# Norm chains moved behind the block boundary, and unread matmuls in TensorE's waits

## What is computed

```python
a = rms_norm(h, g) * (1 + scale) + shift        # before each of the four sub-layers
layer 0: h += gate * rwkv7_mixer(a)             # bidirectional linear recurrence, 16 heads
         h += gate * swiglu(a', w1, w3, w2)     # d_ff 2816, latent and context tokens
layer 1: h += gate * gqa_attention(a)           # 8 query heads, 2 key heads, rotary
         h += gate * swiglu(a', w1, w3, w2)     # latent tokens only
rms_norm(x, g) = x * rsqrt(mean(x * x) + 1e-6) * g
```

## Time and profile before

| | |
|---|---|
| median of 3 runs | 2176.03 us (2170.07 to 2177.54) |
| profiled execution | 2173.98 us, its span 2172.1 us |
| TensorE matmul busy | 1988.3 us (92%) |
| VectorE (DVE) busy | 1230.3 us (57%) |
| ScalarE (ACT) busy | 836.8 us (39%) |
| GpSimd (POOL) busy | 379.3 us (17%) |
| mean granted TensorE clock | 0.963 of 2.4 GHz |

### The profile page before, as it was taken

How to read it: one execution, slowest core, us unless ns; L and a number is a source line. 1 busy time by engine, 2 the same in 40 slices (tenths; PEclk the granted TensorE clock), 3 DMA queues, 4 the chain that set the end, 5 groups by cost and what they waited for, 6 DMA issues and landing times. The chain is left out here.

```text
span 2172.1 us, 52627 instructions
## 1 busy us (share of the span) xinstructions
PE 1988.3 (92%) x22423; PEld 1739.4 (80%) x22423; DVE 1230.3 (57%) x1921; ACT 836.8 (39%) x1407; POOL 379.3 (17%) x394
## 2 busy tenths in 40 slices
PE   5799997789999988979999999997979898999998
PEld 3688886678888887979999999996635476888887
DVE  4765445667767763458756667564775434333333
ACT  2433334565565532344323324233335424422321
POOL 0000000766766652120000000022200010000000
PEclk8799998899999999989999999997989998999999
DMA  9577775101111001411212222212100023333332
GB/s 318 180 239 231 228 237 144 41 19 39 32 39 39 20 12 47 151 59 59 78 59 78 63 74 69 68 39 69 59 20 1 0 68 96 96 105 89 96 107 79
DMA packets 226985, 192.76 MB, mean 89 GB/s; under 512 B 13386, under 2 KB 211668, under 8 KB 226388
## 3 DMA queue, kind: packets, MB, share of 16 engines
q1 hardware_dynamic: 226452, 188.84, 28.1%
q0 software_dynamic: 320, 0.79, 0.2%
HBM read 171.38 MB, written 17.43 MB: 87 GB/s over the span
## 5 line engine op out<-in xcount | busy, mean ns | idle before, releaser
L539 DVE TENSOR_TENSOR ffn_lo<-ffn_raw,ffn_hi 128x1024 fp32r<-128x1024 f32 (+1 forms) x58 | 77.5, 1336 | 196.0 <-ACT ffn_hi L534 196.0
L563 PE MATMUL banks<-operand_hi,ffn_w_hi 128*128 128x384 f32 x464 | 155.7, 336 | 10.9 <-DVE operand_lo L505 10.9
L563 PE MATMUL banks<-operand_lo,ffn_w_hi 128*128 128x384 f32 x464 | 155.6, 335 | 0.0
L563 PE MATMUL banks<-operand_hi,ffn_w_lo 128*128 128x384 f32 x464 | 155.5, 335 | 0.0
L563 PE MATMUL banks<-mix_hi,proj_hi 128*128 128x386 f32 (+1 forms) x384 | 136.9, 356 | 15.4 <-DVE proj_lo L755 10.5
L563 PE MATMUL banks<-operand_hi,ffn_hi 128*128 128x512 f32 x352 | 138.4, 393 | 10.7 <-DVE operand_lo L505 8.4
L534 ACT CAST ffn_hi<-ffn_raw 128x1024 fp32r<-128x1024 f32 (+1 forms) x60 | 68.3, 1139 | 189.6 <-PE banks L563 182.6
L563 PE MATMUL banks<-operand_lo,ffn_hi 128*128 128x512 f32 x352 | 137.9, 392 | 0.0
L563 PE MATMUL banks<-operand_hi,ffn_lo 128*128 128x512 f32 x352 | 137.9, 392 | 0.0
L430 POOL TENSOR_TENSOR mix_and_norm<-mix_and_norm 128x768 f32<-128x768 f32 (+1 forms) x21 | 34.8, 1659 | 572.4 <-ACT mix_and_norm L424 572.4
L563 PE MATMUL banks<-mix_hi,proj_lo 128*128 128x386 f32 (+1 forms) x384 | 132.0, 344 | 0.0
(11 more groups left out here) (341 smaller groups left out, 5681.4 us busy)
## 6 DMA issues: line engine op xcount, KB each, us to landing
mod_raw<-in_mod_w SPq DMA_DIRECT2D x96, 512.0 KB, 5.2
ffn_raw<-in_ff_w SPq DMA_DIRECT2D x32, 1024.0 KB, 5.3
ffn_raw<-in_ff_w SPq DMA_DIRECT2D x46, 512.0 KB, 3.8
ffn_raw<-in_ff_w SPq DMA_DIRECT2D x16, 704.0 KB, 4.7
proj_raw<-in_rw_wr SPq DMA_DIRECT2D x16, 256.0 KB, 5.3
proj_raw<-in_rw_wk SPq DMA_DIRECT2D x16, 256.0 KB, 6.1
proj_raw<-in_rw_wv SPq DMA_DIRECT2D x16, 256.0 KB, 6.1
rwkv_out_raw<-in_rw_wo SPq DMA_DIRECT2D x8, 512.0 KB, 4.2
```

What stands on the lines that cost most here:

```text
L539: signal(eng, eng.tensor_tensor(self.lo[s][:, 0:k_tiles, :], self.raw[s][:, 0:k_tiles, :], self.hi[s][:, 0:k_tiles, :].bitcast(F32), ALU.s ...
L563: mm = pe.matmul(out, a, b, start=(first and n == 0), stop=(last and n == 2), skip_group_check=onto)
```

## The change

A helper `fill` issues matmuls of 256 columns (`ident` as the weight, the constant `cond` as the moving operand) into a PSUM bank whose content nobody reads. It is called at the places below, 134 matmuls in all: 8 and seven times 2 in the first tile of `rwkv_inputs`, 8 at its end; 18 after the first tile's `kk_sum` and 12 after its `bonus_sum`; 4 and 2 in the readout, 4 at the end of `rwkv_out`; in each of the three norms 2 between the groups of sums, 2 behind them and 8 behind the spread; 4, 2 and 10 in the last two steps of `qkv`, 4 at its end; 4 at the end of `attend`, 4 at the end of `dense`.

The chain from `last_square` to `spread` is taken from the end of `rwkv_out`, `feed_forward_seven` and `dense` and put at the head of `feed_forward_seven`, `qkv` and `feed_forward`. The sums now always use bank 0. In `feed_forward_seven` POOL waits for its own block's sums before it clears the running sum for the next norm. POOL's running sum has seven of the eight tiles in both kernels.

```diff
@@ -103,6 +103,12 @@
 def half(h):
 
     return slice(CH * h, CH * h + CH)
+
+
+def fill(c, pe, bank, count):
+
+    for _ in range(count):
+        pe.matmul(c.bank[bank][:, 0:256], c.ident[:], c.cond[:].rearrange("p k r -> p (k r)")[:, 0:256], start=True, stop=True)
 
 
 class Core:
@@ -438,23 +444,26 @@
 
         act.activation(self.x[:, 2, self.at0:], self.h[:, CT - 1, self.at0:], ACT.Square).then_inc(self.squared, 1)
 
-    def sums(self, pe, bank):
-
+    def sums(self, pe):
+
+        bank = self.c.bank[0]
         pe.wait_ge(self.pooled, CT * (self.number + 1))
         for n, i in enumerate(self.blocks):
             pe.matmul(bank[:, n:n + 1], self.pool_sum[:, i * P:(i + 1) * P], self.c.ones[:, 0:1], start=(n == 0), stop=False,
                       skip_group_check=True)
+        fill(self.c, pe, 7, 2)
         pe.wait_ge(self.squared, self.tiles + CT)
         for n, i in enumerate(self.blocks):
             mm = pe.matmul(bank[:, n:n + 1], self.x[:, 2, i * P:(i + 1) * P], self.c.ones[:, 0:1], start=False, stop=True,
                            skip_group_check=True)
         mm.then_inc(self.summed, 1)
-
-    def root(self, act, bank):
+        fill(self.c, pe, 7, 2)
+
+    def root(self, act):
 
         n = len(self.blocks)
         act.wait_ge(self.summed, self.number + 1)
-        act.activation(self.rows[:, 0:n], bank[:, 0:n], ACT.Sqrt, scale=1.0 / D, bias=self.c.eps[:, 0:1])\
+        act.activation(self.rows[:, 0:n], self.c.bank[0][:, 0:n], ACT.Sqrt, scale=1.0 / D, bias=self.c.eps[:, 0:1])\
             .then_inc(self.rooted, 1)
 
     def invert(self, dve):
@@ -471,6 +480,7 @@
             at = i * P if i < CTX // P else i * P - CTX
             mm = pe.matmul(out[:, at:at + P], self.rows[:, n:n + 1].to_broadcast([P, P]), self.c.ident[:], start=True, stop=True)
         mm.then_inc(self.spread_done, 1)
+        fill(self.c, pe, 7, 8)
 
     def spread_of(self, at):
@@ -725,6 +735,8 @@
                     need(pe, evac_ctx, n - 1)
                     for k in range(CT):
                         part, j = 2 * n + k // HALF_K, k % HALF_K
+                        if n == 0:
+                            fill(c, pe, 2, 2 if k else 8)
                         if j == 0:
                             pe.wait_ge(w_rest, w_at + part + 1)
                         if i == 0:
@@ -743,6 +755,7 @@
                             if at == k:
                                 low(step)
                 mods.turn(pe, len(batches) - 1)
+                fill(c, pe, 7, 8)
 
             @block.vector
             def _(dve):
@@ -1800,6 +1813,8 @@
                         elif name == "kk_sum":
                             after(pe, use, 0, "kk_square", "sigmoid0")
                             mm = self.sum_tokens(bank, tmp)
+                            mm.then_inc(features["pe"], 1)
+                            return fill(c, pe, 1, 18)
                         elif name == "kk_spread":
                             after(pe, use, 0, "kk_invert", "sigmoid1")
                             mm = self.spread(bank, norm_k)
@@ -1809,6 +1824,9 @@
                                 for b in range(2):
                                     mm = pe.matmul(tokens_of(bank)[half(b), at:at + width], c.ones_head[half(b), half(b)],
                                                    tmp[half(b), at:at + width], start=True, stop=True)
+                            mm.then_inc(features["pe"], 1)
+                            after(pe, use, 0, "sigmoid2")
+                            return fill(c, pe, 4, 12)
                         mm.then_inc(features["pe"], 1)
 
                     def feature(self, t, name):
@@ -2220,11 +2238,13 @@
                     for at, width in SEGS:
                         mm = pe.matmul(gate_out[:, at:at + width], gate_w[:], hidden[:, at:at + width], start=True, stop=True)
                     mm.then_inc(pe_done, 1)
+                    fill(c, pe, 3, 4)
                     pe.wait_ge(act_done, ACT_STEP["square"])
                     for i in range(TOK // P):
                         mm = pe.matmul(sum_out[:, 2 * i:2 * i + 2], gated[:, i * P:(i + 1) * P], c.ones_head[:, 0:P:CH],
                                        start=True, stop=True)
                     mm.then_inc(pe_done, 1)
+                    fill(c, pe, 3, 2)
                     pe.wait_ge(dve_done, DVE_STEP["invert"])
                     for i in range(TOK // P):
                         for b in range(2):
@@ -2249,8 +2269,7 @@
 
                 readout()
                 by_two(pe, 0, CT // 2, pair)
-                norm.sums(pe, c.bank[6])
-                norm.spread(pe)
+                fill(c, pe, 7, 4)
 
             @block.scalar
             def _(act):
@@ -2286,9 +2305,6 @@
                 act.wait_ge(added, ns * (CT - 1))
                 norm.square(act, CT - 2, 0)
                 norm.table(act)
-                act.wait_ge(added, ns * CT)
-                norm.last_square(act)
-                norm.root(act, c.bank[6])
 
             @block.gpsimd
             def _(pool):
@@ -2343,7 +2359,6 @@
                     pair(i)
                 add(CT - 2, 0)
                 add(CT - 1, 1)
-                norm.invert(dve)
 
 
 def dense(c, name, weight, hi, lo, segs, h, layer, gate_row, norm, raw):
...
@@ -2532,6 +2542,8 @@
                                                   (g_hi[:, k, g], g_lo[:, k, g]), k == 0, k == HT - 1)
                         mm.then_inc(w.product, 1)
 
+                norm.sums(pe)
+                norm.spread(pe)
                 halves(pe, tile, outputs)
 
             @block.scalar
@@ -2568,6 +2580,8 @@
                         if isinstance(j, int):
                             finish(half, HT - 1, 0, s)
 
+                norm.last_square(act)
+                norm.root(act)
                 halves(act, tile, outputs)
 
             @block.gpsimd
@@ -2627,6 +2641,7 @@
                         elif s == 1:
                             multiply(half, HT - 1, 0)
 
+                norm.invert(dve)
                 norm.scale(dve, 0)
                 halves(dve, tile, outputs)
                 for s in range(2):
...
@@ -3087,12 +3097,10 @@
                         act.wait_ge(added, 3 * (self.of("added", PARTS - 1, m)))
                         following.square(act, m, m % 2)
 
-                act_part = Act()
-                schedule(act_part)
+                norm.last_square(act)
+                norm.root(act)
+                schedule(Act())
                 following.table(act)
-                act.wait_ge(added, 3 * act_part.of("added", PARTS - 1, CT - 1))
-                following.last_square(act)
-                following.root(act, sum_bank(act_part))
 
             @block.gpsimd
             def _(pool):
@@ -3100,6 +3108,7 @@
                     x = pieces[n]
                     pool.wait_ge(rounded, n + 1)
                     nc.gpsimd.tensor_tensor(w_lo[n][:], source(x), w_hi[n][:].bitcast(F32), ALU.subtract).then_inc(rest, 1)
+                pool.wait_ge(norm.summed, norm.number + 1)
                 following.clear(pool)
                 for m in range(CT - 1):
                     following.accumulate(pool, m, m % 2)
...
@@ -3300,6 +3311,8 @@
                                                   (hi[:, kt, at:at + width], lo[:, kt, at:at + width]),
                                                   kt == 0, kt == CT - 1)
                         mm.then_inc(w.product, 1)
+                    if n == NH:
+                        fill(c, pe, 7, 4)
                     if there(n - 1):
 
                         pe.wait_ge(squared, n)
@@ -3312,6 +3325,8 @@
 
                         if isinstance(n, int) and n == KV_HEADS:
                             pe.wait_ge(tables, 48)
+                        if n >= NH:
+                            fill(c, pe, 7, 2 if n == NH else 10)
                         pe.wait_ge(normed, n - 1)
                         need(pe, rotated, n - 2)
                         for b in range(2):
@@ -3487,6 +3506,7 @@
                 values(HEADS - 2, 4, 6)
                 turn(TILES - 1)
                 values(HEADS - 1, 0, T)
+                fill(c, pe, 0, 4)
 
             @block.scalar
             def _(act):
...
```

20 lines of the change are left out of this document (6 added, 14 removed).

## The result

| | before | after |
|---|---|---|
| median | 2176.03 us (2170.07 to 2177.8, 5 runs) | 2160.4 us (2157.24 to 2161.38, 5 runs) |
| ratio | | 0.993, 95% interval 0.9918 to 0.9943 |
| span of the profiled execution | 2172.1 us | 2155.5 us |
| mean granted TensorE clock | 0.963 | 0.989 |

The account below looks back on a forecast made before the run. TensorE was taken to bound the kernel, losing time in waits and at a 1.2 GHz clock after them. The terms summed to -17.1 us from a 2176.03 us median: 2158.9, stated as 2158 us, range 2150 to 2169.

Parts of the forecast that it names:

- First head: First norm chain, moved behind the barrier: first product 4.4 us earlier, 2.2 if the clock falls halfway; taken as 3.3 gain.
- Second head: Second norm chain, moved behind the barrier: first product at 1484.1 to 1486.9 instead of 1490.85; gain taken as 5.0 us.
- Third head: Third norm chain: first product 1793.6 instead of 1796.95, then a full-clock start; gain 2.5 to 6, taken as 4.7 us.
- Projections: Start of the projections' block: fills raise the clock for last products and modulation, nothing is late; gain 1.4 us, bounds 0 to 2.
- Opening: Recurrence opening: end fills start ACT and DVE 0.6 us earlier, 18 and 12 fills are free; gain 0.6 us.
- Readout: Before the output projection: four fills without cover push the sum, ACT's root and DVE's subtraction back; loss 1.4 us, bounds 0.5 to 3.4.
- End of queries, first scores: Last two swaps at full clock -1.8, end fills +0.2, attention's first scores -1.4: sum -3.0 us, bounds -3.3 to +1.
- Dense: Attention to dense: four fills shrink the gap from 4.4 to 2.7 us before 1.2 GHz products; -0.5 us, bounds 0 to -2.
- (a): Rival: the clock falls in the norm chains and stays low there; -10.9 us in all, 2165 us; chance 20%.
- (b): Rival: early weights bring nothing in the heads, because scaling starts no earlier; -5 to -6 us, 2171 us; chance 7%.
- (c): Rival: a fill costs 0.85 us wherever it stands, making the kernel slower; together +13 us, 2189 us; chance 5%.
- (d): Rival: fills do not raise the granted clock at all, some cold fills are exposed; about 2170 us; chance 6%.

Follow-up runs that it names:

- k2: The kernel before with the three norm chains moved behind the barrier as in the change, and no fill anywhere: 2165.8 us, ratio 0.9946.
- k6: The changed kernel without the 22 fills in the projections' first tile and the six in the readout: 2149.91 us, ratio 0.9883 to before.
- k4: The kernel before with the chains moved and the norm's own fills (2, 2 and 8), no others: 2164.16 us, ratio 0.9943.
- k8: Changed kernel without in-chain, first-tile projection and readout-chain fills; POOL held in queries; 20 opening fills, not 12; two and three before output projection steps: 2147.77 us.
- k3: The kernel before with all fills that stand outside the normalization, chains where they were: 2176.06 us, ratio 1.0.

## Why the prediction was right, and where its terms were not

The time was forecast within 2.4 us, by terms of which one had the wrong sign and two were too small.

*First head* (forecast -3.3, 4.4 at most). Measured -4.6 in the one profile, just past the bound, and -3.2 in the other; the difference is the clock in the chain (spread 1.50 and 2.77 us). The spread ended 6.63 us behind the addition, forecast 6.65. (The forecast's terms from barrier to spread add up to 6.3 us, and it used 6.0, which is what was measured.) The step "the fills inside the chain eat what the start won" holds: without them, with the spread at 1.2 GHz, the spread ended at 6.85 and the product came after 12.75 (k2). What ends the wait at the full clock is DVE, which scales until 9.9 and takes 2.41 us for `operand_lo` beside POOL. The weights came 1.0 us later than reckoned (ACT's first cast 6.46 us behind SP's issue, 5.44 before) without harm: in k6 the cast came 1.3 us earlier and the product at the same 12.27.

*Second head* (-5.0). -5.8 and -4.9. What the sum left out is the work behind it: TensorE worked at 1.2 GHz until 1496 before and at the full clock after, which is half of the 3.2 us by which "qkv" is shorter. From the first product to the last of the queries it took 102.4 us before and in k2, 100.8 in after and in k4, which has the norm's fills alone.

*Third head* (-4.7). Gap -3.6, work behind it -1.4: together -5.0.

*Projections* (-1.4, bounds -2 to 0). Wrong in sign: +3.2 in the block, +1.1 in front of it. The step that failed is "TensorE has no operand wait behind it, so 1.4 us go through". The 1.4 us did arrive at the second unit (39.5 us behind the block's start instead of 40.9), and were gone at the fourth (66.1 against 66.4): the block waits for DMAs again and again, with a DMA share of 0.72 between 84 and 360 us before. Over all profiles the six with the eight fills took 309.8 to 311.5 us (mean 310.4), the eight without 305.1 to 308.9 (mean 306.9). Why the loads then come 3 us later than without fills is open. In these two profiles SP issues them at nearly the same distances up to 228 us into the block (227.9 after, 227.5 before), and the wait behind that issue takes 1.96 us instead of 0.36. The means of the six and the eight profiles show a loss that grows in steps: the same load is issued 0.1 us earlier with the fills at 107 us, 0.6 later at 187, 1.1 at 216, 2.5 at 238 and 3.5 at 261. The +1.1 us in front of the block is another matter: the opening's barrier is passed 0.41 to 0.42 us behind the landing of one load (`residual<-x_channels`, 3 MB) in all fourteen profiles, and 0.8 to 3.5 us behind the last work of TensorE; that load took 15.3 us in after, 14.3 before.

*Opening* (-0.6). -0.2; in the noise. The 18 fills ended 12.3 us behind the block's start (worked out: 12.15), and the spread was done before DVE came.

*Readout* (+1.4). In this profile ACT's root came 0.2 us earlier, since the clock happened to be high, which looks like a miss. The seven profiles with the fills have it 6.54 to 9.25 us (mean 8.2) behind the block's start, the seven without 6.42 to 7.26 (mean 6.9): +1.3. Up to the root the uncovered fills cost what the forecast said. In the whole block they cost about 1.1 us (84.6 in the mean of the seven, 83.5 in the five that have no fill at all there), less than the block varies by itself (81.6 to 84.8).

*End of queries, first scores* (-3.0). Queries -1.6 behind their last product, scores -1.35. *Dense* (-0.5, at best -2). -2.1 here and 47.0 us in k6 and k8, -0.5 (48.6) in most others: with four fills before the gap of 2.68 us the clock behind it was 1.00 in three profiles and 0.59 to 0.65 in eight; without them the gap was 4.38 us and the clock 0.50 in all three.

*Rivals.* (a), the clock falling in the chains, came true in part: in the second head in every profile with fills in its chain, in the first in some; by the first head of the changed kernel's two profiles it costs 1.4 us. (b) falls: DVE's first scaling does start 0.3 us later behind the addition than before (6.66 against 6.33), as (b) supposed, and the product comes 4.6 us earlier all the same. (c) falls: 0.43 us. (d) falls with the windows above. POOL and DVE decide by the later of the two, as assumed; no scaling was stretched.

So the total was right partly by luck, because errors cancelled: projections 5.7 us worse than their term, the work behind the second head, dense, the two first heads some 5 us better.

## What to carry to other kernels

Move what is serial and thin behind the barrier and start the next block's loads first: that made 12 of the 16 us, and it adds no work. In this kernel an unread matmul was worth its place only where TensorE waited anyway and real work at a low clock followed at once: 1.6 us at the end of the queries, 1.35 at the first scores, 1.6 behind the second head. In the block that waits for DMAs, and where the wait was already over, it only cost (here 4 to 5 us and about 1), so each place has to be tried by itself. And one profile per kernel can mislead: the output projection's fills look like a gain of 1.4 to 2.9 us until the profile of before is laid beside them.

## What was not expected of the hardware

- A block whose early work is sped up by fills ended 3.5 us later (mean of 6 and 8 profiles), its loads coming later; the longest block without the eight fills (308.9 us) is shorter than the shortest with them (309.8), so this is the program's doing, and it is not explained. Its first DMA issue, too, came later although the fills stand behind it (53.45 to 53.68 us in five of the six, 52.58 in k3; 52.37 to 52.68 in all without). That follows the landing of one load; why this is late in five of the six is open.
- The recurrence took 494.7 to 505.9 us with the same work. TensorE's idle time there that no semaphore explains goes along with it: 17.1 us in the shortest, 23.8 in the longest.
- Twelve one-column sums (24 records) with fills among them leave the clock to chance: the spread behind them took 1.50 us in one profile of the changed kernel and 2.77 in the other, at the second head 2.12.
